# The order of 32 experts in a mixture-of-experts step: three emptiest first instead of experts 0 and 1 first

## What is computed

```python
logits = (h @ router_w).astype(jnp.float32) + router_b       # 520 tokens, 32 experts
top_vals, top_idx = lax.top_k(logits, TOP_K)                 # 4 experts per token
gates = jax.nn.softmax(top_vals, axis=-1)
counts = jnp.bincount(flat_e, length=N_EXPERTS)              # 2080 pairs over 32 experts
...
def expert_block(args):                                      # one expert, its tokens
    xb, e = args
    gu = xb @ w_gate_up[e] + b_gate_up[e]                    # 1024 -> 2048
    g = jnp.minimum(gu[:, :D_FF], SWIGLU_LIMIT)
    u = jnp.clip(gu[:, D_FF:], -SWIGLU_LIMIT, SWIGLU_LIMIT)
    act = (u + 1) * g * jax.nn.sigmoid(SWIGLU_ALPHA * g)
    return act @ w_down[e] + b_down[e]                       # 1024 -> 1024
```

## Time and profile before

| | us |
|---|---|
| median of 3 runs | 1751.74 |
| fastest, slowest run | 1747.32, 1753.02 |
| the profiled execution | 1746.44 |
| its span (first to last instruction) | 1744.8 |
| busy: PE (matmul), DVE, ACT, POOL | 1463.2, 794.1, 339.8, 96.1 |
| DMA: 598.62 MB, mean over the span | 343 GB/s |

### The profile page before, as it was taken

The page is one execution under the profiler, slowest core; times in us unless marked ns, Lnnn a source line. Parts: engine busy times, 40 slices in busy tenths (PEclk is TensorE's granted clock), DMA queues, the critical chain, the costliest instruction groups (busy, mean ns, idle before and its releaser), DMA issues.

```text
span 1744.8 us, 31990 instructions
## 1 busy us (share of the span) xinstructions
PE 1463.2 (84%) x11950; PEld 584.4 (33%) x11951; DVE 794.1 (46%) x1168; ACT 339.8 (19%) x782; POOL 96.1 (6%) x173
## 2 busy tenths in 40 slices
PE   2868856778878968999999999998899899898870
PEld 2434422225534343333333333332333232332220
DVE  2699998896777344211312322232132131131316
ACT  1211112222321220111211211211212122121220
POOL 1000020000000000000000100000000000000000
PEclk9989976889988967999999999999999999999995
DMA  9366579999988775579999999999999999999976
GB/s 335 123 197 187 181 272 335 330 330 311 346 292 293 281 304 213 237 312 394 428 417 405 428 397 414 428 414 400 413 415 414 396 428 401 397 427 428 427 324 251
DMA packets 127180, 598.62 MB, mean 343 GB/s; under 512 B 20263, under 2 KB 20277, under 8 KB 101914
## 3 DMA queue, kind: packets, MB, share of 16 engines
q1 hardware_dynamic: 109088, 560.72, 81.3%
q10 hardware_dynamic: 8522, 20.00, 3.3%
q0 software_dynamic: 9504, 17.06, 2.6%
HBM read 589.88 MB, written 25.87 MB: 353 GB/s over the span
## 4 chain that ended last, share of the span: by engine, by line
PE 39%; DMA 20%; DVE 2%; issue 1%; ACT 0%; DVEq 0%; SPq 0%; ACTq 0%
PE bank L1453 23%; DMA wts<-in_w_gate_up 14%; PE bank L1490 8%; DMA wts<-in_w_down 6%; PE bank L1472 4%; DVE v_ring L2091 1%; PE bank L1443 1%; PE bank L1560 1%; PE bank L1501 1%; PE bank L1541 0%; DVE q_b L2091 0%; DMA h_tok<-h_rows,v_tok 0%; ACT k_T L1104 0%; DVEq L2079 0%; ACT k_T L1087 0%
## 5 line engine op out<-in xcount | busy, mean ns | idle before, releaser
L1453 PE MATMUL bank<-wts,h_T 128*32 128x512 f32 x4032 | 444.1, 596 | 17.9 <-DMA wts<-in_w_gate_up 17.9
L2013 DVE TENSOR_SCALAR q_T<-bank 128x512 f32<-128x512 f32 x32 | 22.1, 692 | 636.3 <-PE bank L1453 636.3
L1490 PE MATMUL bank<-wts,k_T 128*32 128x512 f32 x2048 | 229.8, 599 | 10.5 <-issue 5.7
L1453 PEld LDWEIGHTS bank<-wts,h_T 128*32 128x32 f32 x4032 | 128.9, 111 | 318.4 <-issue 288.9
L1472 PE MATMUL bank<-wts,h_T 128*32 128x512 f32 x992 | 130.1, 666 | 45.0 <-DMA wts<-in_w_gate_up 43.2
L1600 DVE TENSOR_TENSOR wts<-wts,q_b 128x1024 f32<-128x1024 f32 x128 | 158.6, 1239 | 13.2 <-DMA wts<-in_cache_k 7.6
L1603 DVE TENSOR_REDUCE sc<-wts 128x16 f32<-128x1024 f32 x128 | 156.2, 1220 | 4.4
L1094 ACT ACTIVATE h_T<-bank 128x512 f32<-128x512 f32 x66 | 35.9, 595 | 572.1 <-PE bank L1443 572.1
L1490 PEld LDWEIGHTS bank<-wts,k_T 128*32 128x32 f32 x2048 | 64.8, 111 | 153.2 <-issue 140.4
L1165 PE MATMUL bank<-wts,h_T 128*8 128x128 f32 (+1 forms) x480 | 87.6, 438 | 20.5 <-DVE u_tok L1600 13.2
L1104 ACT ACTIVATE k_T<-bank 32x256 f32<-32x256 f32 x256 | 95.7, 374 | 14.6 <-PE bank L1490 11.3
(11 more groups left out here) (323 smaller groups left out, 1360.7 us busy)
## 6 DMA issues: line engine op xcount, KB each, us to landing
wts<-in_w_gate_up SPq DMA_DIRECT2D x126, 2048.0 KB, 17.4
wts<-in_w_down SPq DMA_DIRECT2D x64, 2048.0 KB, 19.3
wts<-in_cache_k SPq DMA_DIRECT2D x256, 256.0 KB, 3.6
v_ring<-in_cache_v SPq DMA_DIRECT2D x128, 256.0 KB, 4.1
wts<-in_cache_v SPq DMA_DIRECT2D x128, 256.0 KB, 4.2
wts<-in_w_in SPq DMA_DIRECT2D x5, 2048.0 KB, 23.6
wts<-y_rows SPq DMA_DIRECT2D x4, 2048.0 KB, 15.2
wts<-in_w_out ACTq DMA_DIRECT2D x1, 4096.0 KB, 17.4
```

Of the source, the lines that this page charges most:

```text
L1453: m = nc.tensor.matmul(PS[part][p0:p0 + 32, :], lhs[:, 32 * b:32 * b + 32], rhs[:, part * F + half * 512:part * F + half * 512 + 512], sta ...
L1490: m = nc.tensor.matmul(PS[4][p0:p0 + 32, :], act_T[0][:, k, a0:a0 + 32], chunk[c][:, k, n * 512:(n + 1) * 512], start=(c == 0 and k == 0), ...
```

## The change

The three emptiest experts come first, then the fullest, then emptiest and fullest of the rest in turn. Written with the rank (0 is the fullest, 31 the emptiest), the places 0, 1 and 2 go to the ranks 31, 30 and 29. The fullest goes to place 3, the second fullest to 5, and so on to 31; the empty ones go to 4, 6, ... 30.

The weights of E0 and E1 must be sent for before the counts are complete. So these two are chosen from the counts of the first three prompt tiles. A new part `S` does this in two steps, one ahead of the rest of the sample attention and one behind the start of `R` of tile 4. It ranks the experts, writes places 0 and 1 of `e_tab` and `col_tab`, and pulls the keys of the two chosen ones to the low end (`EARLY`), so that the later full ranking leaves them at places 0 and 1. SP sends for no expert's weights before this.

```diff
+            sp.wait_ge(meta_out, 1)
+            e, e1 = expert_at(0), expert_at(1)
             sp.wait_ge(fold_done, 2 * CT)
-            load_chunk(1, 0)
+            load_chunk(1, e)
             sp.wait_ge(pv_done, NB * NG)
-            load_chunk(0, 0)
-            load_chunk(3, 0)
+            load_chunk(0, e)
+            load_chunk(3, e)
...
             def gather(i, first):
                 ...
-                V.link(nc.gpsimd.tensor_copy(g_idx, slot_tok[:, bass.ds(column(i, first), 1)]))
+                V.link(nc.gpsimd.tensor_copy(g_idx, slot_tok[:, bass.ds(column(i), 1)]))
...
+            def part_s(_s):                       # PE
+                pe.wait_ge(gT_copied, TILES - 1)
+                nc.tensor.matmul(O[:, 4 * E:5 * E], ones[:, :], chosen_sum, start=True, stop=True).then_inc(counts_done, 1)
+                yield
+                pe.wait_ge(order_done, 1)
+                nc.tensor.matmul(O[0:E, 2 * E:3 * E], ones[0:E, 0:E], ahead, start=True, stop=True)
+                nc.tensor.matmul(O[0:1, 3 * E:3 * E + 2], col_e, early, start=True, stop=True
+                                 ).then_inc(order_placed, 1)
+                yield
...
             transpose_x(0)
-            pe.wait_ge(meta_out, 1)
+            pe.wait_ge(meta_out, 2)
             pe.wait_ge(bias_split, 1)
             expert_block(0)
-            pe.wait_ge(meta_out, 2)
...
+            def part_s(_s):                       # DVE
+                dve.wait_ge(counts_done, 1)
+                nc.vector.tensor_copy(c0, O[:, 4 * E:5 * E]).then_inc(counts_read, 1)
+                rank_experts(1)
+                nc.vector.tensor_scalar(early, iota_e[0:E, 0:2], place_e, None, ALU.is_equal).then_inc(order_done, 1)
+                yield
+                dve.wait_ge(order_placed, 1)
+                V.link(nc.vector.tensor_copy(e_tab[:, 0:2], O[0:1, 3 * E:3 * E + 2]))
+                nc.vector.tensor_copy(col_tab[:, 0:2], O[0:1, 3 * E:3 * E + 2]).then_inc(meta_out, 1)
+                for j, pull in ((0, 2 * EARLY), (1, EARLY)):
...
+            def place_experts():
+                V.link(nc.vector.tensor_scalar(odd_place, rank_e, -2.0, float(2 * E - 4), ALU.mult, ALU.add))
+                V.link(nc.vector.tensor_tensor(odd_place, odd_place, place_e, ALU.max))
+                V.link(nc.vector.tensor_scalar(place_e, rank_e, 2.0, 3.0, ALU.mult, ALU.add))
+                V.link(nc.vector.tensor_tensor(place_e, place_e, odd_place, ALU.min))
...
                 if u == TILES:
                     first_tables()
+                    rank_experts(2)
+                    place_experts()
```

More of the change, by code:

```diff
@@ L33 @@
 UNUSED = 1 << 20
-FIRST_KEY = float(1 << 16)
+EARLY = float(1 << 16)
 LIMIT, ALPHA = 7.0, 1.702
@@ L201, in hybrid_step @@
         col_key, col_e, col_n, key_e, rank_e, odd_place, place_e = [v_tok[0:E, 1, 448 + n:449 + n] for n in range(7)]
+        early, early_row = v_tok[0:E, 1, 130:132], v_tok[0:E, 1, 132:132 + E]
         col_tab = v_tok[0:1, 1, 460:460 + TCOLS].bitcast(i32)
@@ L276, in hybrid_step @@
         plan(("R", 3), 0, 0, values=2)
+        plan(("S", 0), 0)
         SCHEDULE.append((None, ALL, ALL))
         plan(("R", 4), 0)
+        plan(("S", 0), 0)
         plan(("O", 0), 0, 0)
@@ L568, in _ @@
             for c in range(4, 6):
-                load_chunk(c, 0)
+                load_chunk(c, e)
             for c in range(2, 4):
                 sp.wait_ge(w_full[c], 16)
-                load_chunk(c, 1, first_gu)
-            def expert_at(i):
-                return sp.value_load(e_tab[0:1, bass.ds(i, 1)], min_val=0, max_val=E - 1)
+                load_chunk(c, e1, first_gu)
             for c in range(2):
                 sp.wait_ge(w_used[c], 1)
-                load_chunk(c, 1)
+                load_chunk(c, e1)
             sp.wait_ge(meta_out, 2)
@@ L589, in _ @@
                 load_chunk(c, e)
-            load_down(1, 1)
+            load_down(1, e1)
             with sp.Fori(3, E) as i:
@@ L689, in _, with column @@
             pool.reg_mov(rows_0, 0)
-            def column(i, first):
-                return 0 if first else pool.value_load(col_tab[0:1, bass.ds(i, 1)], min_val=0, max_val=TCOLS - 1)
+            def column(i):
+                return pool.value_load(col_tab[0:1, bass.ds(i, 1)], min_val=0, max_val=TCOLS - 1)
             def gather(i, first):
@@ L710, in scatter @@
                     pool.wait_ge(y_scattered, i * 16)
-                V.link(nc.gpsimd.tensor_copy(y_idx, slots[:, bass.ds(column(i, first), 1)]))
+                V.link(nc.gpsimd.tensor_copy(y_idx, slots[:, bass.ds(column(i), 1)]))
                 pool.reg_add(bound, rows_0, PAIRS - 1)
@@ L718, in _ @@
             pool.wait_ge(k, n)
+            pool.wait_ge(meta_out, 1)
             gather(0, True)
+            gather(1, False)
             pool.wait_ge(meta_out, 2)
-            gather(1, False)
             gather(2, False)
@@ L1570, in down_block @@
                 by_size(front, back, i, size)
-            pe.wait_ge(order_done, 1)
+            pe.wait_ge(order_done, 2)
             nc.tensor.matmul(O[0:1, 0:E], col_e, place, start=True, stop=True)
@@ L1797, in first_tables, with rank_experts @@
                                         ).then_inc(slots_done, 1)
[L1798 to L1802, removed]
+            def rank_experts(done):
+                dve.wait_ge(counts_read, done)
                 V.link(mul(ahead, c0[0:E, :], ident[0:E, 0:E]))
@@ L1815, in order_experts, with part_s @@
-                V.link(nc.vector.tensor_copy(col_tab[:, 1:E], O[0:1, 1:E]))
-                nc.vector.tensor_scalar(n_tok[:, 1:E], O[0:1, E + 1:2 * E], float(CAP), None, ALU.min
+                V.link(nc.vector.tensor_scalar(place_e, rank_e, -1.0, float(E - 1), ALU.mult, ALU.add))
+            def part_s(_s):
+                dve.wait_ge(counts_done, 1)
+                nc.vector.tensor_copy(c0, O[:, 4 * E:5 * E]).then_inc(counts_read, 1)
+                rank_experts(1)
+                nc.vector.tensor_scalar(early, iota_e[0:E, 0:2], place_e, None, ALU.is_equal).then_inc(order_done, 1)
+                yield
+                dve.wait_ge(order_placed, 1)
+                V.link(nc.vector.tensor_copy(e_tab[:, 0:2], O[0:1, 3 * E:3 * E + 2]))
+                nc.vector.tensor_copy(col_tab[:, 0:2], O[0:1, 3 * E:3 * E + 2]).then_inc(meta_out, 1)
+                for j, pull in ((0, 2 * EARLY), (1, EARLY)):
+                    V.link(nc.vector.tensor_scalar(early_row, O[0:E, 2 * E:3 * E], float(j), -pull, ALU.is_equal, ALU.mult))
+                    V.link(add(row_key, row_key, early_row))
+                    V.link(nc.vector.scalar_tensor_tensor(col_key, early[:, j:j + 1], -pull, col_key, ALU.mult, ALU.add))
+                yield
@@ L1817, in order_experts, with place_tables @@
+            def place_tables():
+                dve.wait_ge(order_placed, 2)
+                V.link(nc.vector.tensor_copy(e_tab[:, 2:E], O[0:1, 2:E]))
+                V.link(nc.vector.tensor_copy(col_tab[:, 2:E], O[0:1, 2:E]))
+                nc.vector.tensor_scalar(n_tok[:, 0:E], O[0:1, E:2 * E], float(CAP), None, ALU.min
                                         ).then_inc(meta_out, 1)
```

26 lines of the change are left out of this document (10 added, 16 removed).

## The result

| | before | after |
|---|---|---|
| median, us | 1750.68 | 1757.53 |
| fastest, slowest run | 1746.29, 1755.8 | 1752.36, 1763.03 |
| runs | 20 | 20 |
| ratio of the medians, 95% interval | | 1.004 [1.0029, 1.0051] |
| the profiled execution, its span | 1746.44, 1744.8 | 1757.88, 1756.2 |

So the change costs 6.9 us where I had forecast a gain of 6.9. The time lies outside my range.

A forecast was written before the change was run, and what follows sets the result against it. PE was taken to set the pace up to about 756 us, the weight loads from there. The terms -26.5 + 16.1 + 1 + 2.5 = -6.9 us took 1751.7 to 1744.8 us, range 1735 to 1754 us.

The forecast's parts named there:

- Term 1, PE's sum from E0 to E3: PE's work from the first gate-up matmul until the fourth expert frees its first chunk: 90.5 us, next chunk issued at 761.3.
- Together 24.8: PE's forecast time in us for the second expert: front, low clock, transposes, down of the first and activation transposes.
- Together 23.3: PE's forecast time in us for the third expert: front 14.17, then 1.09, 6.87 and 1.16.
- The 1.5 us that I had put at E1: Allowance for the low clock in the second expert's front, on top of 14.17 us.
- Term 1, the stream: Continuous weight loads: 166 chunks instead of 172 at 5.30 us each, without a gap; with PE's sum, -26.5 us.
- Term 2, the end: Last gate-up chunk to the end of the last down: 45.8 us instead of 29.6 with a large last expert, +16.1 us.
- Term 3, the start: Start before the first expert: new part free, +1 us for the gather's column read, +2.5 for meeting early weights.
- no one waits for it: Claim that the 2.7 us ranking, now ahead of the sample's last additions, delays nothing.
- The rivals: Alternatives: start eats the gain, about 1750 us (0.27); end costs nothing extra, 1728.7 (0.08); early weights too late, 1757.3 (0.10).
- The slower one: Rival: first experts' weights wait for the tables, start costs 16 us, 5.6 us slower at 1757.3 us; chance 0.10.
- a gap in the loads after 800 us: Sign that would make the forecast wrong on the slow side.
- no gap in the loads from about 765 us: Sign expected if the forecast held: weight loads follow one another from there on.

The follow-up runs named there:

- E31: Not a follow-up run: the expert at the last place, 31; small in the kernel before, large in the changed kernel.
- e1: Kernel before with only the change's order, its first two experts written in as constants, weights sent for as early as before; 1749.68 us, ratio 1.0013 to before.
- e2: Changed kernel without the back pass's code for gate and up of the first two experts and the down of the first; 1746.59 us, ratio 0.9989 to before.
- e4: Kernel before with places 26 (large) and 31 (small) exchanged, so the last expert is large; 1764.01 us, ratio 1.0098 to before.
- e5: Changed kernel with places 4 and 31 exchanged, so place 4 is large and the last one small; 1746.01 us, ratio 0.9979 to before.
- e7: Changed kernel with the edits of e5 and e2 together; 1734.50 us, ratio 0.9910 to before.
- e3: Changed kernel with its new start and late weights, but the order of before, two large experts first; 1753.42 us, ratio 1.0037 to before.
- e6: Changed kernel with places 2 and 31 exchanged, so place 2 is large and the last one small; 1745.91 us, ratio 0.9980 to before.

## Why the prediction was wrong

- **Term 1, PE's sum from E0 to E3: the failed step.** "Together 24.8" and "Together 23.3" for E1 and E2 leave out that PE stops where it jumps over code, and that its clock is low afterwards. E0 took 24.6 us, as forecast, and E3 17.9 instead of 17.8. E1 took 26.2 and E2 27.1 without their stops, 5.2 us more than forecast, nearly all in two fronts of 16.84 and 16.20 us and one down of 8.66, and the stops are 10.96 us. Together 16.1 of the 16.3 us by which the line is off. I had taken the durations of the earlier trace rows, where each expert runs at least one back pass. The trace of before had one small sign: in its chain a wait of 0.74 us by issue at 771.21 us, in the down of E1, the first in the loop's code, where the second back pass is jumped over. The only jump over both passes in code that had not run yet was the down of E31, whose code is its own. PE waits for ACT there anyway, and hardly a price shows: E31's down starts 1.17 us behind ACT's last copy before, and 0.92 in the change, where its back pass runs. e1 shows the stops come with the order alone, e2 that the largest goes with the code.
- **The low clock is not all the stops'.** The 1.5 us that I had put at E1 for it were right in kind: in e2 the same front takes 16.19 us without a stop, 2.0 over 14.17. The stop of 4.88 us adds only 0.7 to that (16.84). In E2's front and the down of E1, where the clock was at full speed before, the stops cost 2.0 and 1.8 us of it.
- **Term 1, the stream.** From the issue of E4's first chunk to the take-up of the last, 166 chunks took 883.65 us, which is 165 x 5.30 and 9.2 more. Before, 172 chunks took 917.13, which is 171 x 5.30 and 10.8 more. So there is no gap, and the part was right: 33.5 us gained instead of 31.8.
- **Term 2, the end.** 45.0 us instead of 45.8, and e4 gives +15.4 us for it by itself. Right in the sum; inside it, the low clock falls on the back pass (6.37 us instead of 3.6) and not on the front (7.04 instead of 10.03).
- **Term 3, the start.** `S` itself costs nothing on the path, as forecast. That "no one waits for it" is not quite so for the full ranking and its tables: in the change E0's front waits last for DVE (released by L2040 at 678.16 us) and starts 4.07 us behind the transposes' start instead of 3.76, so 0.3 us. POOL's copy is 0.9 us later (666.50 less 4.2 against 661.46), and the gather, which was to be 2.5 us later by the early weights, is 2.6: 7.1 us from issue to use instead of 4.5. The two rows of the changed kernel, POOL's and PE's timeline:

```profile
667.60 1.23 POOL L701 DMA_INDIRECT h_tok<-h_rows,v_tok  x1 [0.92 <-POOL v_tok L699]
...
674.71 1.97 PE L1457 MATMUL bank<-ident,h_tok 128*128 128x128 f32 x8 [6.48 <-DMA h_tok<-h_rows,v_tok]
```

That it is 2.6 so exactly is partly luck: with the same early weights the gather takes 5.6 us in e5, 5.9 in e7, 6.2 in e2 and 7.8 in e3, that is 1.1 to 3.3 us more than before. e3 gives +4.8 us by the medians for the whole start (its interval, 0.24% to 0.50%, is 4.2 to 8.7 us). By the rule of the Trainium skill I had expected a cost nearer to 1 us than to 6 (no figure of the page), and all of these are; no run shows the turns of the queues themselves.
- **The rivals.** None named this. The slower one (early weights too late) was not it: they came at 626 us, as forecast. Its time of 1757.3 us meets the measured one by luck, since it wanted a start 16 us later, and the start came 3.8 later. My signs did point at the failure: "a gap in the loads after 800 us" did not occur, but my other, "no gap in the loads from about 765 us", was broken at 780 to 785 us.

What stays open: why a packet moves when it does, and whether the stream of weights, whose queue fills 96.4% of the DMA engines' time in the third stop, makes it late. Against it stands that the longest of the change's stops, the first, has the weights' queue at 46.2% of the engines' time only, and that the 2.4 to 2.5 us behind the packet are the same in both. It could be tried by holding the weights back there; it wasn't. The parts also don't add to the microsecond: e2's edit is worth 9 us on the change and 11.5 on e5.

## What to carry to other kernels

Where a size decides between long pieces of straight code, the order of the data also decides which code is jumped over the first time. Price that at up to 5 us for each large jump in code that has not run (0.4 to 4.9 in the change), plus up to 2 us of low clock afterwards, and let the first items of a loop be those that run the code through, or give them code without the piece. A slow item belongs neither at the start of a stream bound by memory nor at the very end; the best place for it is where loads hide it, and on this kernel the losses at both ends together (3.8 + 21.6 + 15.4 = 40.8 us by the table of the result) were more than the 33.5 that the order saved.

## What the runs showed that I had not expected

- A jump over both back passes of gate and up, in code not yet run, stops PE for 4.5 to 5.1 us at E1 (4.88 in the change, 4.46 in e1, 5.08 in e5, 4.90 in e6). In the loop's code, run for the first time, it stops PE for 1.1 to 2.9 us in E2's front, and in the down of E1 for 1.5 to 4.2. At E0, where PE waits for its data anyway, no such stop shows: 1.47 us behind ACT in e1 against 1.14 before. A jump over one pass costs 0.74 us in the down of E1 before and 0.54 in e3, and nothing in gate and up of E0 and E1 or in the down of E0.
- The 136 records of a front take 14.17 us at full clock and 16.84 behind the stop of 4.88. Not all of these 2.7 us are the stop's: in e2, without it, the same front took 16.19. The clock is low there (0.50 at 703 to 709 us in e2) since the late table and the transposes ahead of it, in the kernel before too, where PE had not been idle.
- The versions that beat both kernels for any counts are e5 and e6, at -4.7 and -4.8 us, 0.2%. With the code of the first two places cut for experts of at most 64 tokens, e7 comes to -16.2 us, but it would need another way for larger ones.
